# Order of the weight loads in a convolution stage: third and fourth chunk before the output weights and the next expert block

## The chip, the core and the metric

The kernel runs on one core of a Trainium2 chip. The metric is the device time of one execution in microseconds (us), the median of three runs. The core has a matrix engine (PE, TensorE; its weight loads are listed as PEld), a vector engine (DVE), a scalar engine (ACT), a general engine (POOL, GpSimd) and SP, which here does nothing but issue loads and stores. 16 DMA engines move the data.

## The reference, cut to what matters

A two-layer encoder works on 576 tokens (512 of a prompt, 64 of a running stream) of width 1024, in float32. Layer 0 mixes tokens by attention, layer 1 by a convolution module, and each is followed by a mixture of experts with 32 experts of width 256, of which each token uses two. The convolution module is the stage that the change is in:

```python
hid = xn @ w_pw1 + b_pw1                 # 1024 -> 2048
a, g = jnp.split(hid, 2, axis=-1)
u = a * jax.nn.sigmoid(g)                # the gated product (GLU)
dw = depthwise_conv(state ++ u, w_dw) + b_dw   # causal, 31 taps, each channel alone
z = silu(layer_norm(dw, ln_g, ln_b))
out = z @ w_pw2 + b_pw2                  # 1024 -> 1024
```

(`depthwise_conv` stands for the reference's `lax.conv_general_dilated` with one group per channel.)

## The kernel before, in words

**Order of the stages.** Attention, its projection, router and experts of layer 0, combining of the experts' rows, convolution module, router and experts of layer 1, combining and last norm. There is no scheduler. Each engine has its own program, written out by hand, and the programs meet at semaphores. All weights are streamed from HBM by SP, in the order in which SP's program issues them, on one hardware queue (q1).

**The convolution stage.** The 1024 channels are cut into 8 chunks of 128 (`C` = 8). For each chunk n:

- SP loads its two weight blocks, one for `a` and one for `g`, with `conv_load` (L1488 to L1492): two DMAs of 512 KB each. There are two slots, `wp[0]` and `wp[1]`, in `work`; chunk n uses slot n mod 2, so chunk n + 2 can be loaded when PE is done with chunk n.
- PE multiplies (`glu`, `glu_half`, L1534 to L1548) in two halves of 288 tokens. Each half has 16 matmul calls, listed as 32 matmul records; at its end `glu_mm` goes up by one. PE waits for the weights (`wp_in`, L1546) and for the banks that DVE has read (`glu_done`, L1547).
- ACT takes the sigmoid of `g` (`gate`, L1635) and multiplies for the taps 0 to 10 (`products`, L1650).
- POOL adds these products (L1702) and adds their sum to the result (L1709).
- DVE forms the gated product u (`gated`, L1734 for the first half, L1737 and L1739 for the second) and does the taps 11 to 30 (`taps`, L1749, L1750, L1753, L1761, L1764). The first half of chunk n + 1 is gated in the midst of the taps of chunk n, the second half at their end. In the last chunk PE does eleven of the taps (L1579, L1580).

PE, ACT, POOL and DVE run chunks 1 and up in loops whose body holds two chunks. Chunks 0 and 1 are loaded ahead of the stage (`conv_first`, L1500). After the last chunk come the means and variances (L1574, L1603), normalization and the projection with `w_pw2` (L439), then the router and the experts.

**SP's program around the change** (block of SP, L1820 to L1840). For layer 1, SP calls `conv_first`, loads the gain, router weights and biases (L1824 to L1828), and calls `conv_sync` (L1507). That waits until all rows of layer 0 are combined (`combined`), since `w2` lies where the gathered rows were, and then issues

- `w2`, the output weights of the module: one DMA of 4 MB (L1509);
- `first_loads(sp, 1, 0)`: the first expert block of layer 1, made of gate and up weights (`gu_load`, L1365, two DMAs of 2 MB) and down weights (`dn_load`, L1378, 2 MB), to slot 0 of `ring`;
- in a loop the weights of chunks 2 to 7, each behind a wait for `glu_mm`: chunk n + 2 waits for 2n + 2, which means that PE has ended both halves of chunk n.

Then SP waits for the end of the convolution (L1831) and issues the small load of `b_pw2`, the stores of the convolution state, and the loads for the other experts, each behind waits of its own.

Of the kernel before, what the change touches and what calls it, by code (L numbers as in the profile page):

```python
# [11 lines left out]
P = 128  # L12
# [32 lines left out]
def encoder(nc, x_prompt, x_sample, cache_attn_k, cache_attn_v, cache_conv,  # L45
# [10 lines left out]
    C = D // P  # L56
# [29 lines left out]
    with ExitStack() as ctx:  # L86
# [3 lines left out]
        def sem(name):  # L90
            return ctx.enter_context(nc.semaphore(name))
# [143 lines left out]
        w2 = ring[:, 1, 0:C * D].rearrange("p (c n) -> p c n", c=C)  # L235
# [68 lines left out]
        glu_mm = sem("glu_mm"); sig_done = sem("sig_done"); glu_done = sem("glu_done");   # L304
# [1056 lines left out]
        def gu_load(sp, l, p, which=(0, 1)):  # L1361
            s = p % GU_SLOTS
            for w in which:
                src = (w_gate, w_up)[w]
                sp.dma_start(wgu[s][:, w, :, :, :].rearrange("p e c f -> p e (c f)"),  # L1365
                             src[l, 2 * p:2 * p + 2].rearrange("e (p c) f -> p e (c f)", c=C)).then_inc(base.gu_in[s], 16)

        def gu_part(sp, l, p, w, e, at, end):
            s, src = p % GU_SLOTS, (w_gate, w_up)[w]
            sp.dma_start(wgu[s][:, w, e, at:end, :].rearrange("p e c f -> p e (c f)"),  # L1370
                         src[l, 2 * p + e.start:2 * p + e.stop].rearrange("e (p c) f -> p e c f", c=C)[:, :, at:end, :].rearrange(
                             "p e c f -> p e (c f)")).then_inc(base.gu_in[s], 16)
# [4 lines left out]
        def dn_load(sp, l, p, s):  # L1377
            sp.dma_start(wdn[s].rearrange("p e c n -> p e (c n)"),  # L1378
                         w_down[l, 2 * p:2 * p + 2].rearrange("e (p c) n -> p e (c n)", c=FC)).then_inc(base.dn_in[s], 16)

        def first_loads(sp, l, s):

            if s == 0 and l == 0:
                sp.wait_ge(op_ev, PAIRS + FREE)
                for b in range(2):
                    sp.wait_ge(kv_out[b], 64 * PAIRS // 2 + 16)
            if s == 1 and l == 0:
                dn_load(sp, l, s, s)
            if s == 1:
                def x_store(j):  # L1390
                    sp.wait_ge(normed, TILES * (2 * l + 1) + j + 1)
                    sp.dma_start(x_rows[j * P:j * P + rows[j], :], xf[0:rows[j], j, :]).then_inc(x_out, 16)

                for j in range(TILES - 1):
                    x_store(j)
                sp.wait_ge(proj_mm, 2 * TILES * (l + 1))
                gu_load(sp, l, 1, (0,))
                x_store(TILES - 1)
                gu_load(sp, l, 1, (1,))
                gu_load(sp, l, 2, (0,))  # L1400
                gu_part(sp, l, 2, 1, ONE, 0, UNSHARED)
            if s == 0:
                gu_load(sp, l, 0)
                dn_load(sp, l, s, s)
# [83 lines left out]
        def conv_load(sp, cc, s):  # L1488
            wp1 = w_pw1[0].rearrange("(p c) n -> p c n", c=C)

            for w in range(2):
                sp.dma_start(wp[s][:, w, :, :], wp1[:, :, dyn(w * D + cc * P, P)]).then_inc(wp_in[s], 16)  # L1492
# [13 lines left out]

        def conv_sync(sp):  # L1507
            sp.wait_ge(combined, TILES)
            sp.dma_start(w2, w_pw2[0].rearrange("(c p) n -> p c n", p=P)).then_inc(w2_in, 16)  # L1509
            first_loads(sp, 1, 0)  # L1510
            with sp.Fori(0, C // 2 - 1) as it:
                for s in range(2):
                    sp.wait_ge(glu_mm, 4 * it + 2 * s + 2)
                    conv_load(sp, 2 * it + s + 2, s)

        def conv_small_pe(pe):
            pe.wait_ge(raw_in, 16 * 6)
# [293 lines left out]
        def _(sp):  # L1811
# [8 lines left out]
            for l in range(LAYERS):  # L1820
                if l == 1:
                    conv_first(sp)
                sp.wait_ge(normed, TILES * (2 * l + 1))
                sp.dma_start(gain[:, 0, :], broadcast(norm_ffn[l])).then_inc(gain_in, 16)  # L1824
                for src, dst in ((w_group[l], router_w[:, :, 0:GROUPS]), (w_router[l], router_w[:, :, GROUPS:RC])):
                    sp.dma_start(dst, src.rearrange("(p c) n -> p c n", c=C)).then_inc(small_in, 16)
                for src, dst in ((b_group[l], router_b[:, 0:GROUPS]), (b_router[l], router_b[:, GROUPS:RC])):
                    sp.dma_start(dst, broadcast(src)).then_inc(small_in, 16)  # L1828
                if l == 1:
                    conv_sync(sp)  # L1830
                    sp.wait_ge(conv_done, C + CONV_LEAD)  # L1831
                    sp.dma_start(b2, broadcast(b_pw2[0])).then_inc(b2_in, 16)
                    sp.wait_ge(last_ev, 1)
                    sp.dma_start(cp_out[0, 0], last_rows[0:STATE, :]).then_inc(out_done, 16)
                    sp.dma_start(cs_out[0, 0], last_rows[STATE:2 * STATE, :]).then_inc(out_done, 16)
                    sp.wait_ge(out_done, 32)
                if l == 0:
                    first_loads(sp, l, 0)
                first_loads(sp, l, 1)
                experts_sync(sp, l)  # L1840
# [127 lines left out]
```

## Time and profile before

| | |
|---|---|
| median of 3 runs | 1268.4 us (1266.51 to 1270.28) |
| the profiled execution | 1271.54 us, of which span 1269.7 us |
| PE busy, mean granted clock | 1075.1 us (85%), 0.933 |
| DVE, ACT, POOL busy | 491.7, 294.2, 269.7 us |
| DMA, mean over the span | 239 GB/s |
| matmuls of the eight chunks (L1539), first and last start | 690.4 and 833.1 us |

The span is the time between the first and the last instruction of the profiled execution. Times below are microseconds from its start. The busy shares are means over the whole execution, so they don't say what bounds one stage; for that, the waits within the stage are read.

### The profile page before, as it was taken

To read this page: it belongs to the slowest core of one execution; us is meant where nothing else is said; L and a number is where in the kernel's file an instruction comes from. 1 tells how busy PE (TensorE), PEld (TensorE's weight loads), DVE (VectorE), ACT (ScalarE), POOL (GpSimd) and SP (SyncE) were. 2 spreads that over 40 slices of the span, in tenths; PEclk is the share of its full clock that TensorE was granted. 3 is DMA by queue.
4 is the path that set the end of the run, shared out by engine and by line. 5 is a ranking of instruction groups with operands and counts; after the bars stand their busy time and mean duration, and the time that the engine had idled before them with its cause. 6 is when DMAs were issued, how large, how long until landed. Compare 5 with 4: busy or idle time off the path is not lost.

```text
span 1269.7 us, 14631 instructions
## 1 busy us (share of the span) xinstructions
PE 1075.1 (85%) x5342; PEld 623.0 (49%) x5342; DVE 491.7 (39%) x1070; ACT 294.2 (23%) x631; POOL 269.7 (21%) x289
## 2 busy tenths in 40 slices
PE   6999999999997888878766889998987988788880
PEld 5777777775545333322325667754545333333320
DVE  3244444444347111110116769995556111111116
ACT  3233232233111111000013535546111100000002
POOL 2000000001002211111033558870003111101033
PEclk9999999999997999888887989999997989998895
DMA  8953322302706999999954932100028999999973
GB/s 273 388 184 110 109 88 79 95 39 94 315 34 262 381 419 420 419 421 421 416 188 121 360 83 66 33 2 24 34 80 302 416 420 421 421 420 420 392 265 131
DMA packets 110287, 303.68 MB, mean 239 GB/s; under 512 B 18440, under 2 KB 65672, under 8 KB 86521
## 3 DMA queue, kind: packets, MB, share of 16 engines
q1 hardware_dynamic: 87977, 254.74, 52.1%
q0 software_dynamic: 22256, 48.22, 10.4%
q8 instruction: 33, 0.54, 0.2%
q14 instruction: 21, 0.17, 0.0%
HBM read 278.34 MB, written 57.12 MB: 264 GB/s over the span
## 4 chain that ended last, share of the span: by engine, by line
PE 56%; DMA 20%; DVE 11%; issue 8%; ACT 3%; another core or an unknown queue 1%; SPq 1%; DVEq 0%; POOL 0%; POOLq 0%
DMA arena<-in_w_up 16%; PE bank L540 10%; PE bank L1224 10%; PE bank L439 7%; PE bank L1243 7%; PE bank L567 4%; DVE bank L1753 2%; PE bank L590 2%; PE bank L1539 2%; DMA work<-in_w_pw 2%; PE bank L606 2%; PE bank L631 2%; PE bank L347 2%; PE bank L1213 2%; PE bank L972 1%
## 5 line engine op out<-in xcount | busy, mean ns | idle before, releaser
L1224 PE MATMUL bank<-ring,work 128*64 128x512 f32 x704 | 172.9, 647 | 31.8 <-DMA ring<-in_w_up 30.0
L1243 PE MATMUL bank<-ring,work 128*64 128x512 f32 x528 | 127.0, 625 | 31.6 <-DVE work L1262 22.5
L1539 PE MATMUL bank<-arena,work 128*128 128x288 f32 x512 | 128.8, 414 | 13.6 <-DMA work<-in_w_pw 10.7
L540 PE MATMUL bank<-arena,ring 128*128 128x288 f32 x512 | 131.9, 412 | 0.3 <-issue 0.3
L1224 PEld LDWEIGHTS bank<-ring,work 128*64 128x64 f32 x704 | 58.8, 149 | 143.3 <-issue 141.2
L1258 DVE TENSOR_TENSOR work<-work,bank 128x256 f32<-128x256 f32 x33 | 13.9, 421 | 293.7 <-ACT work L1254 283.0
L1539 PEld LDWEIGHTS bank<-arena,work 128*128 128x128 f32 x512 | 98.7, 194 | 43.1 <-issue 12.8
L1702 POOL TENSOR_TENSOR ring<-ring 128x606 f32<-128x606 f32 x76 | 103.6, 1363 | 53.5 <-ACT ring L1650 43.9
L540 PEld LDWEIGHTS bank<-arena,ring 128*128 128x128 f32 x512 | 94.9, 190 | 32.9 <-issue 8.3
L439 PE MATMUL bank<-ring,arena 128*128 128x512 f32 x224 | 100.7, 603 | 2.6 <-ACT arena L1686 2.6
L1224 PE MATMUL bank<-arena,work 128*64 128x512 f32 x352 | 87.4, 653 | 16.1 <-DMA arena<-in_w_up 14.3
L1753 DVE SCALAR_TENSOR_TENSOR bank<-work,ring,bank 128x606 f32<-128x606 f32 x129 | 98.9, 847 | 0.0
L1243 PEld LDWEIGHTS bank<-ring,work 128*64 128x64 f32 x528 | 37.5, 142 | 98.3 <-issue 71.1
L1254 ACT ACTIVATE work<-bank 128x256 f32<-128x256 f32 x33 | 12.7, 383 | 282.6 <-PE bank L1224 253.5
L1130 POOL DMA_INDIRECT work<-x_rows,tok_at x32 | 33.0, 1031 | 209.0 <-DVEq L1069 199.9
L1650 ACT ACTIVATE ring<-work,ring 128x606 f32<-128x606 f32 x84 | 65.4, 797 | 36.9 <-POOL ring L1702 36.9
L439 PEld LDWEIGHTS bank<-ring,arena 128*128 128x128 f32 x224 | 42.1, 193 | 51.7 <-issue 49.4
L1224 PEld LDWEIGHTS bank<-arena,work 128*64 128x64 f32 x352 | 29.8, 151 | 72.4 <-issue 72.4
L746 ACT ACTIVATE work<-work,soft 64x192 f32<-64x192 f32 (+4 forms) x80 | 42.6, 533 | 85.8 <-DVE soft L832 85.8
L1134 POOL DMA_INDIRECT y_sorted<-work,slot_at x16 | 15.8, 986 | 208.8 <-DVE work L1270 208.8
L934 POOL DMA_DIRECT2D out<-work x8 | 4.6, 573 | 249.2 <-ACT work L739 249.2
L1134 POOL DMA_INDIRECT y_sorted<-gain,slot_at x16 | 15.9, 993 | 187.6 <-DVE gain L1270 187.6
(257 smaller groups left out, 1330.9 us busy)
## 6 DMA issues: line engine op xcount, KB each, us to landing
ring<-in_w_down SPq DMA_DIRECT2D x32, 2048.0 KB, 24.9
ring<-in_w_gate SPq DMA_DIRECT2D x20, 2048.0 KB, 20.8
ring<-in_w_up SPq DMA_DIRECT2D x20, 2048.0 KB, 27.8
arena<-in_w_gate SPq DMA_DIRECT2D x10, 2048.0 KB
arena<-in_w_up SPq DMA_DIRECT2D x8, 2048.0 KB
ring<-in_w_qkv SPq DMA_DIRECT2D x24, 512.0 KB, 5.9
y_sorted<-gain POOLq DMA_DIRECT2D x8, 1536.0 KB, 5.7
work<-in_w_pw SPq DMA_DIRECT2D x16, 512.0 KB, 5.8
```

The lines of the kernel that those rows point to most:

```text
L439: mm = nc.tensor.matmul(bank[3 + h][0:rows[j], :], act_t[:, c, j * P:j * P + rows[j]], w[:, c, h * HALF:(h + 1) * HALF], start=c == 0, sto ...
L540: mm = nc.tensor.matmul(bank[b][:, 0:HT], wa[s][:, w, c, :], xt[:, c, h * HT:(h + 1) * HT], start=c == 0, stop=c == C - 1)
L567: mm = nc.tensor.matmul(bank[0][:, j * P:(j + 1) * P], xt_tile(c, j), wa[s][:, 2, c, :], start=c == 0, stop=c == C - 1)
L746: ins = nc.scalar.activation(prob[0:q, b, h, 0:nk], prob[0:q, b, h, 0:nk], ACT.Exp, bias=soft[0:q, b, 0, h:h + 1], accum_out=soft[0:q, b, ...
L1130: pool.indirect_dma_start(xe[local % 2], None, x_rows, bass.IndirectOffsetOnAxis(tok_at[:, local:local + 1], 0), bounds_check=TOKENS - 1, ...
L1134: pool.indirect_dma_start(y_sorted, bass.IndirectOffsetOnAxis(slot_at[:, local:local + 1], 0), ysb[local % 2], None, bounds_check=EXPERTS ...
L1224: mm = nc.tensor.matmul(bank[2 + s][rr, :], rows_t[:, c, rr], wgu[g][:, :, e, c, :], start=c == 0, stop=c == C - 1)
L1243: mm = nc.tensor.matmul(bank[5 + h][rr, :], hts[:, c, rr], wdn[s][:, e, c, h * HALF:(h + 1) * HALF], start=c == 0, stop=c == FC - 1)
L1539: mm = nc.tensor.matmul(bank[banks[h][w]][:, 0:GT], wp[s][:, w, c, :], xt[:, c, h * GT:(h + 1) * GT], start=c == 0, stop=c == C - 1)
L1650: nc.scalar.activation(out, u[s][:, m:m + OUTS], ACT.Copy, scale=cvec[s][:, m:m + 1]).then_inc(prod_done, 1)
L1702: pool.tensor_tensor(side[s], side[s], prod[turn(s, m)], ALU.add).then_inc(side_done, 1)
L1753: steps.behind(V.scalar_tensor_tensor(a, src(t), w(t), a, ALU.mult, ALU.add))
```

## The change

`conv_sync` is rewritten. The loop over the chunks is written out (n = 0 to 5) with the same waits: chunk n + 2 is still issued when `glu_mm` has reached 2n + 2. The 4 MB of `w2` and the three DMAs of the first expert block, which were issued ahead of all of them, are now issued after the loads of the third and fourth chunk (chunks 2 and 3) and ahead of those of the fifth. The wait for `combined` stays in front. No other engine's program is touched.

```diff
         def conv_sync(sp):
             sp.wait_ge(combined, TILES)
-            sp.dma_start(w2, w_pw2[0].rearrange("(c p) n -> p c n", p=P)).then_inc(w2_in, 16)
-            first_loads(sp, 1, 0)
-            with sp.Fori(0, C // 2 - 1) as it:
-                for s in range(2):
-                    sp.wait_ge(glu_mm, 4 * it + 2 * s + 2)
-                    conv_load(sp, 2 * it + s + 2, s)
+            for n in range(C - 2):
+                sp.wait_ge(glu_mm, 2 * n + 2)
+                conv_load(sp, n + 2, n % 2)
+                if n == 1:
+                    sp.dma_start(w2, w_pw2[0].rearrange("(c p) n -> p c n", p=P)).then_inc(w2_in, 16)
+                    first_loads(sp, 1, 0)
```

## Rows read from the trace of the kernel before

**Rows 1.** Costliest groups of the page: busy us, mean ns, idle before.

```profile
L1753 DVE SCALAR_TENSOR_TENSOR bank<-work,ring,bank 128x606 f32<-128x606 f32 x129 | 98.9, 847 | 0.0
```

**Rows 2.** Chain that ended last, 650 to 1000 us: start, us, what.

```profile
709.25 25.10 DMA work<-in_w_pw
734.49 11.10 PE bank L1539 x32
...
870.62 22.43 PE bank L439 x48
```

**Rows 3.** Waits, 690 to 860 us: who, for whom, total us, times, longest.

```profile
ACT work L1635 <- PE bank L1539: 19.3, 3, 12.7
...
DVE work L1734 <- ACT work L1635: 10.9, 2, 10.4
...
PE bank L1539 <- DMA work<-in_w_pw: 10.7, 1, 10.7
```

**Rows 4.** Timeline of SP's issues: start us, us, line, what.

```profile
700.62 0.43 SPq L1509 DMA_DIRECT2D ring<-in_w_pw  x1
...
702.26 4.26 SPq L1378 DMA_DIRECT2D ring<-in_w_down  x1
708.47 22.25 SPq L1492 DMA_DIRECT2D work<-in_w_pw  x3
```

**Rows 5.** Timeline of DVE, chunks 1 to 3: start us, us, instruction [idle before <-releaser].

```profile
727.16 0.91 DVE L1749 TENSOR_SCALAR bank<-work,ring 128x606 f32<-128x606 f32 x1
...
746.15 0.52 DVE L1734 SCALAR_TENSOR_TENSOR work<-bank,ring,work 128x288 f32<-128x288 f32 x1 [10.39 <-ACT work L1635]
...
755.40 0.91 DVE L1749 TENSOR_SCALAR bank<-work,ring 128x606 f32<-128x606 f32 x1 [0.43 <-DVE work L1739]
...
763.91 0.51 DVE L1734 SCALAR_TENSOR_TENSOR work<-bank,ring,work 128x288 f32<-128x288 f32 x1
...
772.86 0.91 DVE L1749 TENSOR_SCALAR bank<-work,ring 128x606 f32<-128x606 f32 x1
```

**Rows 6.** Stretches: us, busy PE, PEld, DVE, ACT, POOL, PEclk, DMA share, GB/s.

```profile
708.30:716.00 7.70, 7.70 (x33) 6.04 (x32) 6.90 (x11) 4.77 (x10) 4.20 (x3) 1.00 1.03 423
...
723.80:734.50 10.70, 0.01 (x1) 0.02 (x1) 10.50 (x18) 5.13 (x11) 9.11 (x8) 0.65 1.06 342
734.50:745.60 11.10, 11.10 (x33) 8.32 (x34) 1.26 (x2) 0.00 (x0) 0.39 (x1) 0.72 0.12 33
745.60:753.60 8.00, 8.00 (x34) 6.27 (x34) 7.42 (x12) 5.04 (x8) 6.09 (x5) 1.00 0.00 0
```

**Rows 7.** Stretches of PE's pause, the same columns.

```profile
724.00:728.00 4.00, 0.00 (x0) 0.00 (x0) 3.84 (x9) 1.52 (x5) 3.57 (x4) 0.88 1.00 416
728.00:730.00 2.00, 0.00 (x0) 0.00 (x0) 1.96 (x4) 1.59 (x3) 1.32 (x3) 0.50 1.10 326
```

**Rows 8.** Landing times of L1492's loads, all 16, from issue.

```profile
DMA to landing us min/median/max: 4.0/5.8/25.1
```

**Rows 9.** DMA, 700 to 740 us, in slices of 1 us, and its instruction queue.

```profile
GB/s 61 30 193 238 303 344 422 410 434 418 418 422 406 434 446 410 418 393 451 401 426 426 418 426 418 434 410 401 337 316 286 285 282 261 304 185 22 0 0 0
...
q8 instruction: 1, 0.02, 0.2%
...
router_b<-in_b_group SPq DMA_DIRECT2D x1, 2.0 KB, 4.1
```

**Rows 10.** DMA, 740 to 800 us: every queue that moved anything (packets, MB, share).

```profile
q1 hardware_dynamic: 6240, 3.15, 18.4%
```

**Rows 11.** Timeline of POOL: its first addition in chunks 1 and 3.

```profile
728.97 1.26 POOL L1702 TENSOR_TENSOR ring<-ring 128x606 f32<-128x606 f32 x1 [0.68 <-ACT ring L1650]
...
774.67 1.25 POOL L1702 TENSOR_TENSOR ring<-ring 128x606 f32<-128x606 f32 x1 [0.34 <-ACT ring L1650]
```

**Rows 12.** Timeline of PE: the first expert block of layer 1 is used.

```profile
973.43 7.09 PE L1224 MATMUL bank<-ring,work 128*64 128x512 f32 x32 [0.91 <-ACT work L1249]
```

**Rows 13.** A stretch of the experts of layer 1, columns as in rows 6.

```profile
1040.00:1100.00 60.00, 50.30 (x218) 19.32 (x220) 7.10 (x13) 5.25 (x10) 8.07 (x8) 0.91 1.02 421
```

## The prediction

> **What bounds the kernel now.** I read the chain of waits first, because the change only reorders loads and can matter only where a load is on that chain. In the convolution stage the chain holds one load: the weights of a chunk, 25.1 us from issue to landing, then 11.1 us of PE with 32 matmul records, which is one half chunk [rows 2]. The view of waits says the same from the engines' side: PE waited once for these weights, 10.7 us; ACT waited at most 12.7 us for PE; DVE waited 10.4 us for ACT's sigmoid [rows 3]. That is one stall, handed on three times, and it must be counted once.
>
> Which of the three counts is seen in DVE's timeline. A chunk of taps runs without a gap in steady state: chunk 2 starts at 755.40 and chunk 3 at 772.86, 17.46 us later, and no tap waited anywhere [rows 1, 5]. PE needs about 7.7 to 8.0 us for a half at full clock, so 15.5 to 16 for a chunk [rows 6], and POOL keeps step 1.8 us behind DVE in chunks 1 and 3 alike [rows 5, 11]. So DVE bounds the stage, and the stall costs what DVE loses. Chunk 1 starts at 727.16 and chunk 2 at 755.40, 28.24 us apart [rows 5].
>
> Why the weights were late is in SP's timeline. The load of chunk 2 was issued at 708.47, as soon as its wait let it. But 4 + 2 + 2 + 2 = 10 MB had been issued from 700.62 on, in front of it on the same queue [rows 4]. The queue moved 393 to 451 GB/s from 706 to 728 and then about 285 with the small pieces of the chunk weights [rows 9]. Among all sixteen loads of this line the median is 5.8 us to landing and the worst 25.1 [rows 8]: the 25.1 is queueing.
>
> **Part 1: chunk 2 goes ahead of the 10 MB.** Its wait and so its issue stay at 708.47. The queue is then nearly empty: the last small load before it was issued near 700 and lands in about 4 us [rows 9]. It lands after 4.0 to 5.8 us, behind two issues of about half a us each, so by 715.5. PE is free for it at 723.8, where its idle stretch begins [rows 6], so the slack is 8 us. PE then ends the first half of chunk 2 at 723.8 + 7.75 = 731.6 and ACT's sigmoid is done by 732.1 or a little later, as ACT does its products in between. DVE asked for it at 746.15 - 10.39 = 735.76 [rows 5]. Stall gone: **-10.39 us**. The halving of the clock goes with it: PE's granted clock was 1.00 before its pause and 0.50 by 728 [rows 6, 7], and the half after it took 11.10 us against 8.00 for the next. These 3 us are inside the 10.39, not beside it.
>
> Against this, the turn of DVE's two-chunk loop shows 0.43 us idle at 755.40 [rows 5], and stays. So chunk 1 will take 17.46 + 0.3 (the 0.43 less the usual gap of 0.1), and chunk 2 starts at about 744.9, 10.5 us earlier.
>
> **Part 2: chunk 3.** Issued at 723.8, when PE has ended chunk 1, with an empty queue. Landed by 730. PE wants it at 723.8 + 15.5 = 739.3. No cost, 9 us of cover.
>
> **Part 3: the 10 MB go behind chunk 3, ahead of chunk 4.** w2 will be issued at about 725 instead of 700.62. It is needed when the projection starts, at 870.62 less the gain [rows 2]: over 100 us of cover. The first expert block is used at 973.43 less the gain [rows 12]: over 200 us. The three waits queued behind them on SP are those for chunks 4 and up; issuing the 10 MB held SP until 702.26 + 4.26 = 706.5, 6 us after the first [rows 4], so until 731, ahead of its next wait, which ends at 739.3. No other queue is passed: POOL issues nothing here.
>
> **Part 4: what is late next.** Chunk 4 now stands behind the 10 MB. How long do 1 + 10 + 1 MB take? From above, the stretch before is the same 12 MB in the other order: first issue 700.62, last byte before 737 [rows 4, 9], 36 us. From 723.8 that is 759.8. From below, 10.5 MB (10 x 1.049) at 420 GB/s are 25 us and each chunk 4 us, with 1 us to begin: 757. PE is free for chunk 4 at 739.3 + 15.5 = 754.8, so it will pause 2 to 5 us. Is that paid? DVE gates the first half of chunk n + 1 at 763.91 - 755.40 = 8.51 us into chunk n [rows 5]. Chunk 3 will start at 744.9 + 17.46 = 762.4, so it asks at 770.9. Less 0.54 for the sigmoid and 7.75 for the half, PE must begin by 762.6; if its clock has fallen to 0.50, with 11.1 for the half, by 759.2. The low end is hidden, the high end costs 759.8 - 759.2 = 0.6 us. I take 0, as the 36 us contain a start at 30 to 240 GB/s beside small loads [rows 9].
>
> One rule speaks against this term. The Trainium skill ("DMA: Bandwidth & Descriptors", Where 436 GB/s comes from) says that for loads from HBM the HBM side binds at about 358 GB/s per core. By it 12.6 MB would take 35.1 us and some 2 us to begin, landing at 761; with the clock fallen that is a stall near 1.8 us and a time of 1259.8. The trace disagrees: 423 GB/s over 7.7 us here and 421 over 60 us [rows 6, 13].
>
> **Part 5: SP's loop written out.** The same twelve DMAs and six waits; register work of some 0.1 us per load goes. SP waits between them anyway: 0.
>
> **Does the gain reach the end?** After 755 all SP issues of the stage and beyond wait for PE or DVE, so they move with it. The experts of layer 1 are fed at 421 GB/s [rows 13], which is a bound by DMA, but no byte moves into or out of that stretch: what was prefetched before still is. It starts 10.4 us earlier and lasts as long.
>
> **Sum.** -10.4 + 0 + 0 + 0 against 1271.54 of the profiled execution: 1261.1. That execution was 3.1 above the median, so by the median **1258.0 us**.
>
> **The rivals.**
>
> A. *A second stall at chunk 4* (8%). For it: the 36 us above end only 2.8 us before 762.6. If the clock has fallen and the pair lands 1 to 7 us after 759.2, DVE loses as much: 1259 to 1265. Against: the rate of rows 9.
>
> B. *The same stall, so large that the kernel is slower* (3%). The 12 MB would have to land late enough to lose more than 10.4 us: half clock gives back 3.35, so after 762.6 + 7.05 = 769.6, which is 46 us for 12.6 MB, or 275 GB/s. The nearest row is the end of the queue, 261 to 304 GB/s with the small pieces [rows 9]. At 245 GB/s, below all of them, landing is at 775.1, the stall 12.5 + 3.35 = 15.9, the time 1273.9. It needs the large pieces to run at the small pieces' rate or less; they ran at 420.
>
> C. *A loop turn fetches instructions through busy DMA engines* (3%). The turn of the loops on DVE, ACT, POOL and PE at 739 to 746 now falls into the burst; before, it fell into silence. In 740 to 800 us, which holds two such turns, no instruction packet moved [rows 10], and one that moved in 700 to 740 was waited for by nobody [rows 3, 9]. If one had to be fetched, its price is that of a small load, 4.1 us [rows 9]: 1262. The Trainium skill ("Runtime: NRT & Kernel Launch", Instruction fetch mechanics) holds that a taken branch to a page out of the window costs such a fetch; rows 10 say that these targets are within.
>
> D. *The change gains nothing* (4%): chunk 2 isn't held by the queue but slow by itself, or PE wants something else at 723.8. DVE's banks were free by 727, and other chunks land in 5.8 us; it would leave 1268.4.
>
> **How the numbers follow.** The forecast has 82%. Its own range is 1255.5 to 1260.5: gain 9.8 (a stall of 0.6) to 10.9, and the runs' spread of 1.9. The range given goes to 1262 for C and most of A. A difference under 0.3% (3.8 us) can't be told from none here. Faster: forecast, C and most of A, 92%. Same: D and the end of A, 5%. Slower: B, 3%.
>
> **What would show it.** Right: no wait of PE L1539 for the chunk weights at 724; DVE L1734 of chunk 2 without idle time near 736; L1749 of chunk 2 at 744.9; the granted clock 1.00 from 724 to 750; w2 issued at 725; then a PE pause of 2 to 5 us before chunk 4 that reaches no DVE row; all later stages 10.4 us earlier at equal length. Wrong: an idle time of DVE at 771 (A, B), an idle time above 0.5 us at a loop turn near 745 (C), or PE still waiting at 724 (D).

## The result and the profile after

The changed kernel takes 1258.99 us, the median of four runs (1256.82 to 1262.05), against 1267.91 us for the kernel before, run beside it (1266.51 to 1270.28). The ratio is 0.9936 with a 95% interval of 0.9918 to 0.9954, which is 8.1 us of 1267.9 (5.8 to 10.4). The profiled execution took 1262.05 us with a span of 1259.7, 10.0 below the span of before.

SP's timeline of the changed kernel (start us, us, line, what) answers to [rows 4]:

```profile
708.27 16.72 SPq L1492 DMA_DIRECT2D work<-in_w_pw  x4
725.03 0.89 SPq L1513 DMA_DIRECT2D ring<-in_w_pw  x1
725.96 1.77 SPq L1365 DMA_DIRECT2D ring<-in_w_gate  x1
727.77 1.04 SPq L1365 DMA_DIRECT2D ring<-in_w_up  x1
728.86 2.97 SPq L1378 DMA_DIRECT2D ring<-in_w_down  x1
739.26 55.11 SPq L1492 DMA_DIRECT2D work<-in_w_pw  x8
```

Chunk 2 is asked for at 708.27, as before, but first. w2 follows chunk 3, at 725.03. The next chunk, number 4, is asked for at 739.26 with most of the 10 MB (6 of them) still in front of it. DVE's timeline answers to [rows 5] (columns as there):

```profile
727.09 0.91 DVE L1749 TENSOR_SCALAR bank<-work,ring 128x606 f32<-128x606 f32 x1
735.60 0.51 DVE L1734 SCALAR_TENSOR_TENSOR work<-bank,ring,work 128x288 f32<-128x288 f32 x1
...
744.84 0.91 DVE L1749 TENSOR_SCALAR bank<-work,ring 128x606 f32<-128x606 f32 x1 [0.43 <-DVE work L1739]
...
762.29 0.91 DVE L1749 TENSOR_SCALAR bank<-work,ring 128x606 f32<-128x606 f32 x1
770.80 0.51 DVE L1734 SCALAR_TENSOR_TENSOR work<-bank,ring,work 128x288 f32<-128x288 f32 x1
```

The gating of chunk 2 has no idle time in front of it, where there were 10.39 us. Chunk 2 starts at 744.84 instead of 755.40. Its loop turn cost 0.43 us as before. PE's timeline shows what became late instead:

```profile
698.22 56.53 PE L1539 MATMUL bank<-arena,work 128*128 128x288 f32 x232
759.24 64.88 PE L1539 MATMUL bank<-arena,work 128*128 128x288 f32 x256 [4.49 <-DMA work<-in_w_pw]
```

PE runs through from chunk 0 to chunk 3 and then pauses 4.49 us for chunk 4. Two stretches of that pause (us, busy PE, PEld, DVE, ACT, POOL, PEclk, DMA share, GB/s) and ACT's sigmoid of the half behind it show how near this came to costing something:

```profile
754.80:757.50 2.70, 0.00 (x0) 0.00 (x0) 2.70 (x4) 1.31 (x2) 2.38 (x3) 1.00 1.19 292
757.50:759.20 1.70, 0.00 (x0) 0.00 (x0) 1.70 (x4) 1.09 (x3) 1.54 (x2) 0.52 1.20 291
```

```profile
769.84 0.50 ACT L1635 ACTIVATE work<-bank,ring 128x288 f32<-128x288 f32 x1 [1.78 <-PE bank L1539]
```

The granted clock was 1.00 up to 757.5, 0.52 from there to 759.2 and 0.50 from 759.2 to 764, so the half chunk took 10.60 us (759.24 to 769.84) instead of 7.75. The sigmoid ended at 770.34 and DVE asked at 770.80: 0.46 us to spare.

Two more stretches, in the same columns, show where the time of the burst went:

```profile
725.00:754.00 29.00, 29.00 (x121) 22.75 (x120) 28.30 (x45) 16.17 (x30) 24.77 (x21) 1.00 1.01 397
754.00:759.24 5.24, 0.75 (x4) 0.24 (x3) 5.24 (x8) 3.19 (x5) 4.69 (x4) 0.84 1.16 293
```

By 754.0 the queue had moved 11.5 MB, which is chunk 3 and the 10 MB. The last 5.24 us moved 1.5 MB, but the pair of chunk 4 has only 1.05. SP issued the pair of chunk 5 at 754.8, as soon as PE had ended chunk 3, and no other load is in the queue then. So about 0.5 MB of chunk 5 moved before chunk 4 had landed.

### The profile page after: what moved, and what is told of

The parts are those of the page before. It is cut to its first block, busy times and chain, and to the rows that moved or that the text cites. A ratio compares the mean times of both kernels' runs of the same rounds, so it can differ in the third digit from the quotient of the medians.

```text
span 1259.7 us, 14595 instructions
## 1 busy us (share of the span) xinstructions
PE 1071.2 (85%) x5342; PEld 623.8 (50%) x5342; DVE 491.3 (39%) x1070; ACT 294.7 (23%) x631; POOL 270.7 (21%) x289
## 3 DMA queue, kind: packets, MB, share of 16 engines
q0 software_dynamic: 22256, 48.22, 10.5%
## 4 chain that ended last, share of the span: by engine, by line
PE 56%; DMA 18%; issue 11%; DVE 11%; ACT 2%; POOL 1%; SPq 1%; DVEq 0%; POOLq 0%
DMA ring<-in_w_up 17%; PE bank L1224 12%; PE bank L540 10%; PE bank L439 7%; PE bank L1243 7%; PE bank L567 4%; DVE bank L1753 3%; PE bank L590 2%; PE bank L1213 2%; PE bank L606 2%; PE bank L631 2%; PE bank L347 1%; PE bank L972 1%; DVE arena L333 1%; PE bank L1579 1%
## 5 line engine op out<-in xcount | busy, mean ns | idle before, releaser
L1702 POOL TENSOR_TENSOR ring<-ring 128x606 f32<-128x606 f32 x76 | 103.7, 1364 | 44.9 <-ACT ring L1650 35.3
L1224 PE MATMUL bank<-arena,work 128*64 128x512 f32 x352 | 82.8, 625 | 14.4 <-DMA arena<-in_w_up 13.4
```

What stands on the lines that cost most here:

```text
L1224: mm = nc.tensor.matmul(bank[2 + s][rr, :], rows_t[:, c, rr], wgu[g][:, :, e, c, :], start=c == 0, stop=c == C - 1)
L1702: pool.tensor_tensor(side[s], side[s], prod[turn(s, m)], ALU.add).then_inc(side_done, 1)
```

## The experiments

**How they are read.** An execution's start varies by some us before the stage is reached (the first taps of chunk 0 begin at 705.4 to 709.7 us in the profiles below, in no order). So beside the times, the profiles are compared by two stretches: from DVE's L1749 of chunk 0 to that of chunk 7, which I call the **chunk stretch**, and the time of the **first 48 projection matmul records**. In kernels with lines added or removed the line numbers move by one or more.

### The change repeated, the loop alone, and two other places for the 10 MB

The first kernel is the changed one. The second has the old order with the written-out loop; its edit is shown against the changed kernel, as are the next ones:

```diff
             sp.wait_ge(combined, TILES)
+            sp.dma_start(w2, w_pw2[0].rearrange("(c p) n -> p c n", p=P)).then_inc(w2_in, 16)
+            first_loads(sp, 1, 0)
             for n in range(C - 2):
...
-                if n == 1:
-                    sp.dma_start(w2, w_pw2[0].rearrange("(c p) n -> p c n", p=P)).then_inc(w2_in, 16)
-                    first_loads(sp, 1, 0)
```

The third and fourth have `if n == 0:` and `if n == 5:` in place of `if n == 1:`. Expected:

> The changed kernel again, beside the three below. Theory (DVE lost 10.4 us waiting for chunk 2 behind the 10 MB, and all of it reaches the end): 10 us faster than before, ratio 0.992, DVE's L1749 of chunk 2 at 744.8, a PE pause of about 4.5 us before chunk 4, which ended 0.46 us short of costing DVE anything. Rival (part of the gain is given back by a second stall in some executions): DVE L1734 of chunk 4 idle by some tenths of a us or more, and a spread wider than that of the kernels below without the pause.

> SP's loop written out, but w2 and the first expert block again ahead of all chunks. Theory: the gain is from the order alone, so this is the kernel before: ratio 1.000 within 0.002, DVE idle 10.4 us before the first half of chunk 2. Rival (the written-out loop, with its 36 instructions less, brings part of it): faster than before by some us, with the stall shorter than 10 us.

> The 10 MB are issued after the load of chunk 2 alone, so from 709.5 us on; chunk 3 stands behind them and lands at about 709.5 + 26 + 4 = 739.5, where PE is free for it at 739.3. Theory (the stall was chunk 2's alone; what counts is that each pair lands before DVE's deadline less one half): gain 10.4 us as with the change, ratio 0.992, PE pause under 1 us, none before chunk 4. Rival (chunk 3 is as sensitive as chunk 2 was): a DVE idle time at about 753, time nearer to before.

> The 10 MB are issued after the loads of all chunks, near 785 us. No pair ever stands behind them. Theory: no PE pause for weights at all, DVE as in the changed kernel, same time, ratio 0.992; w2 is in by 810 and needed at 860. Rival (the pause before chunk 4 in the changed kernel still costs): this is faster than the changed kernel by 0.5 to 2 us. Second rival (the transfer at 700 to 750 slowed something else): a difference in the length of chunks 0 to 3.

Measured, against 1265.29 us for the kernel before (17 runs):

| kernel | median us (runs) | ratio, interval | chunk stretch us | PE pause for weights us | DVE idle for it us |
|---|---|---|---|---|---|
| changed, again | 1258.67 (6) | 0.9935, 0.9920 to 0.9950 | 122.73 | 4.51 | 0 |
| old order, written out | 1266.58 (12) | 1.0006, 0.9995 to 1.0017 | 133.98 | 12.41 | 11.18 |
| 10 MB behind chunk 2 | 1259.18 (5) | 0.9947, 0.9934 to 0.9960 | 124.35 | 5.67 | 1.52 |
| 10 MB behind all chunks | 1257.98 (6) | 0.9934, 0.9921 to 0.9947 | 122.73 | 0 | 0 |

The waits of the written-out loop in the old order carry the verdict (who, for whom, total us, times, longest us):

```profile
PE bank L1538 <- DMA work<-in_w_pw: 12.4, 1, 12.4
DVE work L1733 <- ACT work L1634: 11.2, 1, 11.2
```

The stall is there in full without the loop: the order alone is what counts. The repeated change has no DVE idle time at chunk 4, and the kernel in which chunk 4 never waits has the same chunk stretch to 0.01 us, so in these profiles the pause of 4.5 us is free. The equal stretches also say that the 10 MB moving at 725 to 754 us slow nothing else in the chunks. The repeated change had been expected at a ratio of 0.992 and came out at 0.9935, and its runs spread over 4.3 us against 3.8 for the kernel without any pause, so no second stall in some executions shows there.

The kernel with the 10 MB behind chunk 2 alone missed its expectation. I had the pair of chunk 3 land as PE became free; it came 5.67 us later. SP's timeline:

```profile
704.79 1.26 SPq L1492 DMA_DIRECT2D work<-in_w_pw  x2
706.09 0.93 SPq L1513 DMA_DIRECT2D ring<-in_w_pw  x1
...
720.25 70.73 SPq L1492 DMA_DIRECT2D work<-in_w_pw  x10
```

and PE's (below, chunk 3 and up begin at 741.41):

```profile
741.41 79.60 PE L1539 MATMUL bank<-arena,work 128*128 128x288 f32 x320 [5.67 <-DMA work<-in_w_pw]
```

From w2's issue at 706.09 to the use of the pair at 741.41 are 35.3 us, where I had counted 26 + 4 = 30. The count had left out the pair of chunk 2, which was issued at 704.79 and still had to move, and the pair of chunk 4, which SP issued from 735.77 on, before that of chunk 3 had landed. From 704.79 on the stretch is 36.6 us; the changed kernel took 35.4 us, from 723.8 to 759.24, also with 12 MB up to the pair that PE waited for. The rate of 420 GB/s of the full queue can't be taken for such a burst as a whole; the 36 us of the burst before could. DVE lost 1.52 us by it. The ratio, 0.9947, can't be told from the 0.9934 with all chunks ahead.

### How much may stand ahead of chunk 2

The next kernel has the first expert block (6 MB) ahead of chunk 2 and w2 behind chunk 3; the one after it has w2, gate and up (8 MB) ahead and the down weights behind chunk 3:

```diff
             sp.wait_ge(combined, TILES)
+            first_loads(sp, 1, 0)
             for n in range(C - 2):
...
-                    first_loads(sp, 1, 0)
```

```diff
             sp.wait_ge(combined, TILES)
+            sp.dma_start(w2, w_pw2[0].rearrange("(c p) n -> p c n", p=P)).then_inc(w2_in, 16)
+            gu_load(sp, 1, 0)
             for n in range(C - 2):
...
                 if n == 1:
-                    sp.dma_start(w2, w_pw2[0].rearrange("(c p) n -> p c n", p=P)).then_inc(w2_in, 16)
-                    first_loads(sp, 1, 0)
+                    dn_load(sp, 1, 0, 0)
```

> Only the first expert block (6 MB) stands ahead of chunk 2; w2 (4 MB) follows chunk 3. With 10 MB ahead the pair landed at 734.35; 4 MB less at 420 GB/s are 10 us, so 724.4, and PE is free at 723.8. Theory (a stall begins when the pair lands after about 727): PE pause about 0.6 us, DVE idle 0, gain 10.4 us, and no pause before chunk 4, as only 4 MB stand ahead of it. Rival (any large load ahead of chunk 2 costs in proportion to its bytes): gain 0.4 of 10.4, 4 us.

> w2, gate and up (8 MB) ahead of chunk 2, the down weights (2 MB) after chunk 3. The pair lands at 734.35 - 5.0 = 729.4, PE pauses 5.6 us, its clock falls to half as in the 4.5 us pause of the changed kernel, whose next half took 10.6 us: first half of chunk 2 done at 740.0, sigmoid at 740.5, DVE asks at 735.7. Theory: DVE idle 4.9 us, gain 5.5 us, ratio 0.9957. Rival (the clock plays no part): half in 7.75 us, DVE idle 2.0, gain 8.4. Rival in proportion to bytes: gain 2 us.

Against 1266.06 us for before: 6 MB ahead 1257.91 us, ratio 0.9940 (0.9922 to 0.9958), chunk stretch 122.73, no pause of PE for weights at all, where I had expected 0.6 us; 8 MB ahead 1260.14 us, ratio 0.9954 (0.9941 to 0.9966), chunk stretch 126.92. The rows of the second, PE first:

```profile
725.71 71.87 PE L1540 MATMUL bank<-arena,work 128*128 128x288 f32 x288 [5.74 <-DMA work<-in_w_pw]
```

DVE's gating of chunk 2:

```profile
736.04 0.52 DVE L1735 SCALAR_TENSOR_TENSOR work<-bank,ring,work 128x288 f32<-128x288 f32 x1 [4.09 <-ACT work L1636]
```

and ACT's sigmoid ahead of it:

```profile
735.51 0.50 ACT L1636 ACTIVATE work<-bank,ring 128x288 f32<-128x288 f32 x1 [6.39 <-PE bank L1540]
```

PE paused 5.74 us, forecast 5.6. The half behind it took 9.80 us (725.71 to 735.51), 2.05 more than at full clock, and DVE idled 4.09 us, forecast 4.9. So the cost at DVE in this kernel starts somewhere between 6 and 8 MB: 0, 0, 4.1 and 10.4 us for 0, 6, 8 and 10 MB ahead. It is neither in proportion to the bytes nor without the clock's part, which would have left 2.0. The granted clock read 0.50 as the half behind the pause began, here and in the changed kernel. The Trainium skill ("TensorE: Matmul & The Clock Gate", Part 1: The HAM clock gate) says that the clock is set by how busy PE has been lately; these rows agree.

### How late chunk 4 may be

With the 10 MB behind all chunks, a wait delays the load of chunk 4 without the burst. The load of chunk 5 stands behind it in SP's program and is delayed with it. The edit is against the kernel with the 10 MB behind all chunks:

```diff
             for n in range(C - 2):
                 sp.wait_ge(glu_mm, 2 * n + 2)
+                if n == 2:
+                    sp.wait_ge(glu_done, 8 + GLU_LEAD)
                 conv_load(sp, n + 2, n % 2)
```

The other kernel has 7 in place of 8.

> As with all chunks ahead of the 10 MB, but the load of chunk 4 also waits until DVE has gated the second half of chunk 3, at 762.3, so it lands at about 767.3 with an idle queue. Theory (chunk 4 is free up to 762.6, or 759.2 with the clock down, and costs us for us beyond): PE pauses 12.5 us, half in 11.1 us, sigmoid at 778.9, DVE idle 8.1 us at 770.8, gain 10.4 - 8.1 = 2.3 us. Rival (DVE or ACT have slack there that hides more): gain over 6 us.

> As the one before, but chunk 4 waits only for the gating of the first half of chunk 3, at 753.9: it lands at about 759, as in the changed kernel, without any burst. Theory: PE pauses 4 to 4.7 us and the clock falls, DVE idle 0 to 0.3 us, time as with all chunks ahead, ratio 0.992. Rival (the pause costs by itself, through the clock): 1 us or more slower than that one.

Measured: 1264.97 us, ratio 1.0002 (0.9989 to 1.0015) for the late one, 1259.32 us, 0.9943 (0.9920 to 0.9965) for the other. DVE's row of the late one:

```profile
775.25 0.52 DVE L1736 SCALAR_TENSOR_TENSOR work<-bank,ring,work 128x288 f32<-128x288 f32 x1 [7.57 <-ACT work L1637]
```

and of the other:

```profile
768.80 0.52 DVE L1736 SCALAR_TENSOR_TENSOR work<-bank,ring,work 128x288 f32<-128x288 f32 x1 [0.72 <-ACT work L1637]
```

and PE's, in the same order:

```profile
765.25 63.75 PE L1541 MATMUL bank<-arena,work 128*128 128x288 f32 x256 [13.71 <-DMA work<-in_w_pw]
```

```profile
758.21 64.33 PE L1541 MATMUL bank<-arena,work 128*128 128x288 f32 x256 [6.28 <-DMA work<-in_w_pw]
```

Pauses of 4.5, 6.28 and 13.71 us cost DVE 0, 0.72 and 7.57. Both pauses are longer than expected (4 to 4.7, and 12.5). The trace of the second kernel shows why: SP issued the pairs of chunks 4 and 5 one right behind the other, from 751.13 to 753.7, the two together moved 2.1 MB, and chunk 4 could be used at 758.21, 7.1 us after its issue. With all chunks ahead, where the pairs go one at a time, the two issued at 736.9 and 752.4 landed in 4.0 to 5.3 us. So this kernel missed its expectation of 0 to 0.3 us at DVE, and its ratio of 0.9943 is not clear of the 0.9934 without a pause: the rival that the pause costs 1 us or more by itself is neither shown nor excluded by the times.

The deadline model holds: in the late kernel DVE asked at 775.25 - 7.57 = 767.68, so PE had to begin by 767.68 - 0.54 - 7.75 = 759.39; it began 5.86 us later and its half took 9.47, 1.72 more than 7.75; the sum is 7.58. What rivals A and B describe exists, then, and the late kernel has it: the gain is gone, though the change is not at fault. The time is worse than I expected by some 2 us: its chunk stretch of 130.40 is only 1.4 to 3.6 below the four profiles with the stall (next part), and the runs can't tell it from before.

### The 2 to 3 us that the times lack

The chunk stretch fell by 10.5 us between the first two profiles (133.25 to 122.74), but the ratios of the changed kernel give 8.1 and 8.2. PE's timeline at the projection shows a difference between profiles. This is the changed kernel:

```profile
849.39 8.03 PE L1603 MATMUL bank<-arena,mean_w 128*128 128x256 f32 x32 [1.73 <-ACT arena L1679]
860.04 22.50 PE L439 MATMUL bank<-ring,arena 128*128 128x512 f32 x48 [2.62 <-ACT arena L1686]
```

and this the old order with the loop written out:

```profile
857.55 8.03 PE L1602 MATMUL bank<-arena,mean_w 128*128 128x256 f32 x32 [1.73 <-ACT arena L1678]
868.20 20.84 PE L439 MATMUL bank<-ring,arena 128*128 128x512 f32 x48 [2.62 <-ACT arena L1685]
```

The pause of 2.62 us is the same, the 48 records take 22.5 or 20.84 us. The stretches of the changed kernel behind that pause show the clock:

```profile
858.38:860.08 1.70, 0.04 (x1) 0.07 (x1) 1.70 (x6) 1.69 (x3) 0.00 (x0) 0.97 0.00 0
860.08:862.38 2.30, 2.30 (x3) 1.10 (x4) 2.30 (x4) 2.30 (x6) 0.00 (x0) 0.50 0.00 0
```

To test it, the kernel before was profiled once more, and three kernels got matmuls of the identity, which nobody reads, in that pause: before, changed, and the one with the 10 MB behind all chunks.

```diff
             mm.then_inc(var_mm, 1)
+            keep_running(8)
             pe.wait_ge(w2_in, 16)
```

> The kernel before, once more, for a second profile of it. Theory of the missing 2 to 3 us (the profiles show 10.5 us gained in the convolution, the medians 7.3 to 8.9): after the variances PE pauses 2.6 us ahead of the projection, and the clock falls there in some executions only, for 1.6 us; the profiled executions of before and after both had it. Then this profile shows DVE's L1749 of chunk 0 to that of chunk 7 in 133 to 134 us again, and the projection's first 48 matmuls in either 20.8 or 22.4 us. Rival (the convolution of before is shorter in most executions than in its profile): that stretch is below 131 us.

> The kernel before with eight idle-time matmul calls (about 2.1 us) between the variances and the projection, so that PE pauses 0.5 us there. Theory: the clock stays at 1.00 in every execution, the first 48 projection matmuls take 20.8 us; before had the loss in some of its executions, so 0 to 1.6 us faster than before, narrower spread. Rival: the clock falls for the light work of the variances themselves, nothing changes.

> The changed kernel with the same eight calls. Theory: the order of the loads is worth 10.5 us, and what the medians lack is the clock at the projection, so this is 10 us faster than the kernel before with the same calls, and 1.6 us faster than the changed kernel. Rival (the gain is given back elsewhere, behind the router in the experts' stage): the difference to the kernel before with the calls stays at 7 to 8 us, and the stretch from the projection to the end is longer than in that kernel.

> All chunks ahead of the 10 MB, with the same eight calls: no pause of PE for chunk weights, and none ahead of the projection. Theory: as the changed kernel with the calls or up to 0.5 us faster, ratio to before 0.992. Rival: the 10 MB at 785 to 815 us disturb DVE or PE there: slower than that one.

Measured, against 1266.50 us for before (15 runs; its second profile is of one run, 1265.65):

| kernel | median us (runs) | ratio, interval | chunk stretch us | first 48 records us |
|---|---|---|---|---|
| before, second profile | | | 131.83 | 20.84 |
| before, kept busy | 1265.41 (11) | 0.9992, 0.9982 to 1.0002 | 133.65 | 20.84 |
| changed, kept busy | 1255.62 (5) | 0.9915, 0.9901 to 0.9928 | 122.78 | 20.84 |
| all ahead, kept busy | 1255.86 (5) | 0.9919, 0.9905 to 0.9932 | 122.77 | 20.84 |

PE of the changed kernel, kept busy:

```profile
855.10 1.95 PE L1206 MATMUL bank<-ident 128*128 128x128 f32 x16
857.89 20.84 PE L439 MATMUL bank<-ring,arena 128*128 128x512 f32 x48 [0.84 <-ACT arena L1687]
```

With that pause filled, the change is worth 0.9915 / 0.9992 = 0.9923, or 9.8 us, nearer to the 10.9 by which these two stretches differ. From the two intervals I estimate 7.6 to 11.9 us for it, which does not separate it from the 8.1 without the filling.

Without the filling, all the profiles of the changed kernel's kind, with a chunk stretch of 122.7 us, show the slow projection: changed, changed again, 10 MB behind all, 6 MB ahead (22.50 to 22.54). Of the three profiles of the old order without the filling only the first shows it, with 22.43 us [rows 2]; the second profile of before and the written-out loop don't. (The second profile of before missed its expectation of 133 to 134 us for the chunk stretch, too: it has 131.83.) Filling the pause gained the old order 0.8 thousandths, not clear of zero, and took the changed kernel from ratios of 0.9935 and 0.9936 to 0.9915 (intervals that overlap a little, measured beside different runs of before).

The likeliest account is that the change gives back 1.6 us at the projection in most executions, while before pays them in few. What each execution that was only timed did there isn't recorded: that the slow projection is absent in all three profiles with the filling is shown, the share of executions is inferred. Two observations don't fit well. The spread of before, kept busy (5.8 us over 11 runs), is not narrower than that of before (4.6 us over 15), as I had expected. And the kernel with the 10 MB behind chunk 2 and the one with chunk 4 late both have the fast projection in their profiles (20.84 us), yet by their ratios they gain 2.1 and 3.0 us less than their chunk stretches differ from the mean of the four with the stall, 133.2. Their profiled executions were the fastest of five and of ten, so the others may have been different. The cause of the missing 2 to 3 us is argued, not shown.

The stretches also correct the stall: old-order profiles have 131.83 to 133.98 us, with DVE idle 8.95 to 11.18, so 10.39 was a fair draw. The clock makes much of the spread: the two profiles of before have the same pause, 10.71 and 10.78 us, but the half behind it took 11.12 and 9.62.

The rival to this, a gain given back in the experts' stage, is small but not excluded: from the first to the last expert block's first matmul the kept-busy kernels take 249.47 us (before) and 250.21 (changed), a difference of 0.7 inside the 249.5 to 251.8 of all fourteen profiles. The four longest of them, 251.5 to 251.8, all belong to kernels with a changed order.

**The fastest version.** The changed order with the eight calls is faster than before by 10.8 us (ratio 0.9915). The changed kernel's 0.9935 and 0.9936 were measured beside other runs of before, and the intervals overlap, so a gain over the changed kernel is likely but not shown. With all chunks ahead it is the same within the intervals (0.9919), with PE never waiting for chunk weights, so it has no 0.46 us edge to fall from.

## Why the prediction was right

**The forecast of 1258.0 us met 1258.99, and the range holds it.** The sign, the mechanism and its place were right; the gain of 10.4 us came out as 8.1 by the ratio, most likely because a term was missing. That the number is only 1.0 off is in part luck: the medians alone differ by 8.9, and the runs of before beside it came out 0.5 below the 1268.4 that the sum started from.

- *The stall counted once, at DVE: -10.39.* Shown. It is gone in the changed kernel and back in full with the old order in a written-out loop.
- *Chunk 2 starts at 744.9.* It started at 744.84, the loop turn costing 0.43.
- *Chunk 3 free, w2 and the expert block covered.* Shown: no wait for any of them, even with all 10 MB issued behind the last chunk.
- *Chunk 4 lands at 757 to 759.8, and PE pauses 2 to 5 us.* It landed at 759.24, near the upper end, and the pause was 4.49. I took 0 for it, and 0 it was, by 0.46 us, which is luck as much as reasoning: had the half taken 11.12 us, as in the profile of before, DVE would just have begun to wait. The sum for the lower bound is wrong by 0.8: 723.8 + 25 + 4 + 4 + 1 is 757.8, not 757. All but one of these terms held, since chunk 3 and the 10 MB had moved by 754.0, against 753.8 by the sum. The 4 us for the pair of chunk 4 were 5.2, because chunk 5's pair was already moving beside it. The 35.1 us estimated by the Trainium skill's rule ("DMA: Bandwidth & Descriptors", Where 436 GB/s comes from) are near the 35.4 measured, but not for the reason that it states: the queue ran above its 358 GB/s, at about 420, through the large pieces, and lost the time at the beginning and with the small pieces, at 293.
- *Rival A, a second stall at chunk 4.* It did not occur, but a pause 1.8 us longer costs 0.72 us of DVE. With 0.46 us to spare, 8% was a low chance to give it.
- *Rival B, slower.* Not here. Its price held in one part: each us behind the deadline cost one. The clock's part did not: 1.72 us in the late kernel, against the 3.35 of the working.
- *Rival C, the loop turn in the burst.* DVE's turn at 744.84 cost 0.43 as in silence, and from 720 to 760 us no instruction packet moved. It fell.
- *Rival D.* It fell with the first profile.
- *"All later stages 10.4 us earlier at equal length."* This is the step that fell short. In the two profiles compared it holds to 0.5 us, since both have the slow projection, and that hid the flaw. Over the executions 2 to 3 us are missing; 1.6 of them are likely the projection, which is slow in the five profiles without the filling that have the shortest chunk stretch, and in one of three of the old order. The profile of before had the clock at 0.50 behind a pause of 2.62 us in it, and I did not ask whether every execution pays that. The rest stays open.

## What to carry to other kernels

When one queue serves both what is needed next and what is needed much later, put the late loads behind the near ones, and then find the next near load that stands behind them: work out when its consumer's consumer asks, not when the first engine goes idle. Take the time of a mixed burst from a burst of the same size in the trace, not from the peak rate, and check which further loads are issued before it ends, since they take their share of the rate. A gain seen in one stretch of one profile should be checked against the ratio of the times; where they differ by more than the interval allows, look for a stretch whose length differs between profiles of the same program.

## What the runs showed of the hardware that I had not expected

The same 2.62 us pause of PE ahead of the same work was followed by a granted clock of 0.50 in some profiles and of 1.00 in others, 1.6 us apart, and which of the two came went with the length of the chunks before it: all five profiles with a chunk stretch of 122.7 to 123.6 us and no filling had the 0.50, against one of the six others without filling. Eleven profiles are few, and why the length should matter no run here shows. The price of a fallen clock also varied: the half chunk behind a pause took 11.12, 10.60, 10.05, 9.80, 9.53 and 9.47 us behind pauses of 10.71, 4.49, 6.28, 5.74, 5.67 and 13.71 us, so it does not follow the length of the pause. It goes with how long the granted clock still read 0.50 once PE worked again: some 6 us for the 11.12, 5 for the 10.60 and 3 for the 9.47.
